# Rotary embedding: the rotated halves made by ScalarE copies instead of a TensorE product

## The chip, the cores and the metric

The kernel runs on one core of a Trainium2 chip. The metric is the time of one execution on the device, in microseconds (us). TensorE multiplies matrices, DVE (VectorE) does element-wise work and reductions, ACT (ScalarE) activations and scaled copies, POOL (GpSimd) element-wise work, and SP issues DMAs.

## What is computed

One step of an encoder layer for 512 frames of a new stream and 32 of a running one, 544 columns in all. Cut to what matters here:

```
h = rms_norm(x); z = h @ w_in          # columns: GLU a, GLU b, q, k, v, two gates
q = rope(rms_norm(q), pos); k = rope(rms_norm(k), pos)
rope: x1, x2 = halves of 64;  out = [x1*cos - x2*sin, x2*cos + x1*sin]
attention per head with two q/k pairs of width 64, block-causal mask, values of width 128
conv branch, merge with gates, w_out, residual; then a mixer with 16384 single-neuron experts
```

A head's tile holds two vectors of 64 on 128 partitions, so the half that x is paired with lies 32 partitions away: blocks 0 and 1 are exchanged, and blocks 2 and 3, and the even ones get a minus sign.

## The kernel before, in words

Everything lies transposed: channels on partitions, 544 frames along the free axis. The stage that the change touches projects h by w_in, in 72 units of 128 columns, 9 for each of 8 heads: unit 0 is q, 1 k, 2 v, 3 and 4 the GLU halves, 5 to 8 gates. A unit is 96 matmuls (16 blocks of the inner dimension, three products of high and low parts, two halves of 272 frames), written by `product` (L1616) into one of two PSUM pairs PA. Weights pass through three steps: SP loads w_raw, ACT rounds it to w_hi (L719), POOL (or DVE) subtracts to w_lo (L654, L1017). The weights of unit n + 2 are converted while unit n + 1 runs.

All small TensorE work of a head is hung into the units by hand: `head_hooks` (L1728) says behind which quarter of which unit each piece runs. The statistics of the queries run half way through unit 1 and their rotation three quarters through it; those of the keys in the same places of unit 2; the transposes of the values in unit 3; and from the first quarter of unit 3 on the attention steps: scores (L1678), weights_t (L1697), mix_values (L1714). Each waits for semaphores, and since TensorE works in order, a wait there stops the unit too.

A rotary turn, i = 0 for queries and 1 for keys, goes so. DVE evacuates the unit from PSUM to zb (L1060). ACT squares it into sq (L758), scales it by the norm's gain into xg (L759), converts the next weights (L719), and, when TensorE has summed the squares of each block of 64 (`stats`, L1651), takes the root into rstd (`std`, L739), for which the table of functions is changed in turn 0. TensorE multiplies xg by a signed permutation into the PSUM pair TO (`rot`, L1659). DVE's `rope` (L1062) takes the reciprocal of rstd (L1065), multiplies xg by the cosines (L1069), TO by the sines (L1071 to L1073), adds (L1075) and multiplies by rstd into q_t or kn_t (L1081). Between these, DVE transposes a part of the expert table (`turn`, L1020), which SP stores in DRAM (L398); each transpose waits for the store of the one two before it.

In the first three units of a head DVE has two such transposes per unit, later about one. A loop body of ACT, DVE and SP holds a pair of heads (r = 0 and 1). The last step of a head on DVE, `o_norm` (L1133), stands behind its last evacuation; in front of the second head of a pair DVE has one transpose more there than in front of the first. TO is used later in the head by the values and the attention.

Of the kernel before, what the change touches and what calls it, by code (L numbers as in the profile page):

```python
# [23 lines left out]
ACT = mybir.ActivationFunctionType  # L24
AX = mybir.AxisListType

P = 128
# [27 lines left out]
STEPS = QT + 1  # L55
# [27 lines left out]
C_COS, C_SIN, C_ID, C_BLK, C_PERM, C_ONES, C_NEG, C_END = np.cumsum([0, TP, TP, P, P, P, P, 64]).tolist()  # L83
# [29 lines left out]
def build(nc, w_all, x_t, consts, late, params, lams, keys_t, past_k, past_v, hist,  # L113
          y_t, k_t, v_n, cst_p, cst_s):
    ctx = ExitStack()
    with ctx:
# [24 lines left out]
        cst = misc.take("consts_sb", [P, C_END])  # L141
# [14 lines left out]
        xg = ay.take("xg", [P, T])  # L156
# [109 lines left out]
        S, TO = ST[:, 0:2, :], ST[:, 2:4, :]  # L266
# [8 lines left out]
        SV, TOV = S[:, :, 0:HT], TO[:, :, 0:HT]  # L275

        def two(ap):

            return ap.rearrange("p (a b) -> p a b", a=2)
# [27 lines left out]
        zb_full, z_taken = sem("zb_full"), sem("z_taken")  # L307
        sq_ready, stat_ready, std_ready = sem("sq_ready"), sem("stat_ready"), sem("std_ready")
        rot_ready, rot_taken, norm_done = sem("rot_ready"), sem("rot_taken"), sem("norm_done")
# [399 lines left out]
        def _(act):  # L709
# [31 lines left out]
            def z_slot(hp, r, i):  # L741

                h = hp * 2 + r
                n = r * ZPH + i
                j = n % 2
                un = hp * (2 * ZPH) + n

                def next_hi():
                    act.wait_ge(unit_done, un + 1)
                    hi(hp * ZPH + (n // 2 + 1), j)  # L750

                if i >= 5:
                    next_hi()
                act.wait_ge(zb_full, un + 3)
                if i in (0, 1):
                    m = h * 3 + i
                    act.wait_ge(norm_done, m + 1)
                    act.activation(sq[:, :], zb[:, j, :], ACT.Square).then_inc(sq_ready, 1)  # L758
                    act.activation(xg[:, :], zb[:, j, :], ACT.Copy, scale=par[:, P_QG + i:P_QG + i + 1]).then_inc(z_taken, 1)  # L759
                if i == ZPH - 1:  # L760
                    act.wait_ge(conv_done, h + 2)
                    act.dma_start(c_scr[bass.ds(h, 1), :, 0:TP].rearrange("a p n -> p (a n)"), c_run[:, 0:TP]).then_inc(c_stored, 16)
                    act.dma_start(c_scr[bass.ds(h, 1), :, TP:T].rearrange("a p n -> p (a n)"), c_run[:, TP + HIST:]).then_inc(c_stored, 16)
                    act.wait_ge(norm_done, h * 3 + 4)
                    act.dma_start(o_scr[bass.ds(h, 1)].rearrange("a p n -> p (a n)"), o_lo_st[:, :].bitcast(F32)).then_inc(o_stored, 16)
                if i >= 4:
                    act.activation(zb[:, j, :], zb[:, j, :], ACT.Tanh, scale=0.5).then_inc(z_taken, 1)
                if i >= 5:
                    act.wait_ge(z_taken, h * 7 + (i - 1))
                    act.dma_start(gate_scr[bass.ds(h * 2 + ((i - 5) if i < 7 else (KD + i - 7)), 1)].rearrange("a p n -> p (a n)"),  # L770
                                  zb[:, j, :]).then_inc(gate_stored[(i - 5) % 2], 16)
                if i < 5:
                    next_hi()
                if i in (0, 1):
                    act.wait_ge(stat_ready, h * 3 + (i + 2))
                    std(1.0 / DH)

# [38 lines left out]
            with act.Fori(0, NH // 2) as hp:  # L816
                own.loop(hp, per)
                for r in range(2):
                    h = hp * 2 + r
# [162 lines left out]
        def _(dve):  # L982
# [79 lines left out]
            def rope(h, i):  # L1062

                dve.wait_ge(std_ready, h * 3 + (i + 3))
                own.by(V.reciprocal(rstd[:, :], rstd[:, :]))  # L1065
                cs = ((slice(0, TP), slice(0, TP)), (slice(TP, T), slice(PAST, PAST + TS)))
                dve.wait_ge(rot_ready, h * 2 + (i + 1))
                for to, fr in cs:
                    own.by(V.tensor_tensor(xg[:, to], xg[:, to], cst[:, fr], ALU.mult))  # L1069
                s0, t0 = C_SIN, TP - HT  # L1070
                own.by(V.tensor_tensor(sq[:, 0:HT], TO[:, 0, 0:HT], cst[:, s0:s0 + HT], ALU.mult))  # L1071
                own.by(V.tensor_tensor(sq[:, HT:TP], TO[:, 1, 0:t0], cst[:, s0 + HT:s0 + TP], ALU.mult))
                V.tensor_tensor(sq[:, TP:T], TO[:, 1, t0:HT], cst[:, s0 + PAST:s0 + PAST + TS], ALU.mult).then_inc(rot_taken, 1)  # L1073
                dve.wait_ge(rot_taken, h * 2 + (i + 1))
                own.by(V.tensor_tensor(xg[:, :], xg[:, :], sq[:, :], ALU.add))  # L1075
                settle()
                if i == 0:
                    dve.wait_ge(sc_ready, h * STEPS + 1)
                else:
                    dve.wait_ge(k_stored, h * 16 + 1)  # L1080
                V.tensor_tensor((kn_t if i else q_t)[:, :], xg[:, :], rstd[:, :], ALU.mult).then_inc(norm_done, 1)  # L1081
# [397 lines left out]
            i = 0  # L1479
# [133 lines left out]
        def _(pe):  # L1613
# [16 lines left out]

            ident = cst[:, C_ID:C_ID + P]
            blk = cst[:, C_BLK:C_BLK + P]
            perm = cst[:, C_PERM:C_PERM + P]
            ones = cst[:, C_ONES:C_ONES + P]

            def spread(out, m, src, start=True, stop=True):
                for f in range(2):
                    last = mm(out[:, f, 0:HT], m, src[:, f * HT:(f + 1) * HT], start=start, stop=stop)
                return last
# [11 lines left out]
            def stats(h, i):  # L1651

                pe.wait_ge(sq_ready, h * 3 + (i + 1))
                pe.wait_ge(std_ready, h * 3 + (i + 2))
                if i == 2:
                    pe.wait_ge(exp_done, h * STEPS + STEPS + 1)
                spread(S, ones if i == 2 else blk, sq).then_inc(stat_ready, 1)

            def rot(h, i):  # L1659
                pe.wait_ge(z_taken, h * 7 + (i + 1))  # L1660
                if i == 0:
                    pe.wait_ge(o_ready, h * STEPS + 1)
                else:
                    pe.wait_ge(rot_taken, h * 2 + i)
                spread(TO, perm, xg).then_inc(rot_ready, 1)

            def values(h, j):
                pe.wait_ge(zb_full, h * ZPH + 5)
# [57 lines left out]


            def head_hooks(h, r):  # L1728
                at = {(1, 1): lambda: stats(h, 0), (1, 2): lambda: rot(h, 0),
                      (2, 1): lambda: stats(h, 1), (2, 2): lambda: rot(h, 1),  # L1730
                      (3, 1): lambda: values(h, r % 2)}
                slots = [(i, q) for i in range(3, ZPH) for q in range(4)]
                for s in range(STEPS):
                    late = 2 if s == QT - 1 else 0
                    for d, f in ((0, scores), (3 + late, weights_t), (4 + late, mix_values)):
                        key = slots[4 * s + d]
                        old = at.get(key)
                        at[key] = (lambda f=f, s=s, old=old: ((old() if old else None), f(h, s)))
                at[slots[22]] = lambda: stats(h, 2)
                return at  # L1740
# [343 lines left out]
```

## Time and profile before

| | |
|---|---|
| median of 3 runs | 3885.25 us (3883.28 to 3887.92) |
| profiled execution | 3884.83 us, span 3883.0 us |
| TensorE busy | 3784.3 us, 97% of the span, mean granted clock 0.993 |
| DVE busy | 3006.9 us, 77% |
| ACT busy | 1101.9 us, 28% |
| POOL busy | 1341.8 us, 35% |
| projection stage | from 40 to 1065 us |

The span reaches from the first instruction to the last. A matmul's end is modelled, so TensorE's busy share says little of its own; idle time before an instruction and what released it say more. In rows of the timeline the first number is the start in us, the second how long the merged instructions took, and a bracket gives the engine's idle time before them and what ended it. L1638 is the line of a helper that the statistics and the rotation share; the operand tells them apart (sq and xg).

### The profile page before, as it was taken

What the parts mean: (1) busy time and instruction counts of PE and PEld (TensorE: products, weight loads), DVE (VectorE), ACT (ScalarE), POOL (GpSimd) and SP (SyncE); (2) the same over time, 40 slices, a digit from 0 to 9 for tenths busy, and PEclk for the clock granted to TensorE, in tenths of its full rate; (3) what the DMA queues carried; (4) which work ended last, traced back from release to release, by engine and by line L of the source; (5) the groups of instructions that cost most, each with busy time, mean ns of one, the idle gap of its engine ahead of it and who ended that gap; (6) DMA issues with size and microseconds to landing.
All of it is one profiled execution on the core that took longest, in us unless ns stands there. A gap on an engine that the chain in (4) does not pass through costs nothing.

```text
span 3883.0 us, 66565 instructions
## 1 busy us (share of the span) xinstructions
PE 3784.3 (97%) x24903; PEld 3728.2 (96%) x24903; DVE 3006.9 (77%) x3608; ACT 1101.9 (28%) x1120; POOL 1341.8 (35%) x923
## 2 busy tenths in 40 slices
PE   8999999999999998999999999999999999999999
PEld 7999999999899997999999999999999999999999
DVE  6887788778755554588789999997588888887876
ACT  3333333333221112222233333332222222222222
POOL 3433334333435442455542222223033333332320
PEclk9999999999999998999999999999999999999999
DMA  7799888998889997899989999999889989898995
GB/s 275 285 322 330 308 299 297 332 332 292 299 269 300 365 402 266 294 372 357 365 328 389 389 379 388 380 386 394 289 316 346 362 316 357 316 347 317 339 351 193
DMA packets 451705, 1285.55 MB, mean 331 GB/s; under 512 B 34368, under 2 KB 258368, under 8 KB 343360
## 3 DMA queue, kind: packets, MB, share of 16 engines
q1 hardware_dynamic: 372576, 876.99, 63.1%
q0 software_dynamic: 46080, 335.56, 22.0%
q10 hardware_dynamic: 32832, 70.07, 4.7%
q8 instruction: 140, 2.29, 0.2%
q14 instruction: 77, 0.63, 0.0%
HBM read 1070.18 MB, written 345.75 MB: 365 GB/s over the span
## 4 chain that ended last, share of the span: by engine, by line
PE 42%; issue 28%; POOL 13%; DMA 10%; DVE 4%; ACT 1%; SPq 1%; POOLq 0%; DVEq 0%; ACTq 0%
PE ST L1965 18%; PE ST L1888 17%; POOL w_lo L654 13%; DMA w_raw<-w_all 4%; PE PA L1888 4%; DMA u_rows<-u_out 3%; PE ST L1941 2%; DMA rows<-v_rows,v_idx 2%; DVE w_lo L1017 2%; ACT w_hi L719 1%; SPq L492 1%; DVE PA L1525 1%; DMA rows<-u_rows,v_idx 1%; PE PA L1869 1%; DVE u_out L1032 1%
## 5 line engine op out<-in xcount | busy, mean ns | idle before, releaser
L654 POOL TENSOR_TENSOR w_lo<-w_raw,w_hi 128x512 fp32r<-128x512 f32 x588 | 811.4, 1411 | 1129.6 <-ACT w_hi L719 1085.9
L719 ACT ACTIVATE w_hi<-w_raw 128x2048 fp32r<-128x2048 f32 x368 | 703.8, 1913 | 1335.6 <-PE ST L1965 513.3
L1965 PE MATMUL ST<-wt_hi,w_hi 128*128 128x384 f32 x2048 | 687.1, 336 | 13.6 <-DVE w_lo L1017 13.6
L1965 PE MATMUL ST<-wt_lo,w_hi 128*128 128x384 f32 x2048 | 685.4, 335 | 0.0
L1965 PE MATMUL ST<-wt_hi,w_lo 128*128 128x384 f32 x2048 | 685.4, 335 | 0.0
L1017 DVE TENSOR_TENSOR w_lo<-w_raw,w_hi 128x2048 fp32r<-128x2048 f32 x219 | 501.1, 2288 | 175.3 <-ACT w_hi L719 168.0
L690 POOL DMA_INDIRECT rows<-v_rows,v_idx x160 | 322.8, 2017 | 738.5 <-DVE PA L1525 669.0
L1626 PE MATMUL PA<-h_hi,w_hi 128*128 128x272 f32 x2496 | 536.5, 296 | 4.3 <-DVE w_lo L1017 4.3
L1626 PE MATMUL PA<-h_hi,w_lo 128*128 128x272 f32 x2496 | 518.6, 289 | 0.0
L1626 PE MATMUL PA<-h_lo,w_hi 128*128 128x272 f32 x2496 | 516.8, 289 | 0.0
L1888 PE MATMUL ST<-h_hi,w_hi 128*128 128x384 f32 x1408 | 508.4, 361 | 1.2 <-DVE w_lo L1017 1.2
L1888 PE MATMUL ST<-h_hi,w_lo 128*128 128x384 f32 x1408 | 475.3, 338 | 0.0
L1888 PE MATMUL ST<-h_lo,w_hi 128*128 128x384 f32 x1408 | 473.4, 336 | 0.0
L1626 PEld LDWEIGHTS PA<-h_hi,w_hi 128*128 128x128 f32 x2496 | 395.5, 189 | 23.1 <-issue 17.6
L1965 PEld LDWEIGHTS ST<-wt_hi,w_hi 128*128 128x128 f32 x2048 | 385.4, 188 | 18.0 <-DVE w_lo L1017 17.7
L1525 DVE SCALAR_TENSOR_TENSOR PA<-rows,w_g,PA 128x2048 f32<-128x2048 f32 x158 | 371.2, 2350 | 37.2 <-DMA rows<-v_rows,v_idx 36.8
L1626 PEld LDWEIGHTS PA<-h_lo,w_hi 128*128 128x128 f32 x2496 | 394.1, 189 | 0.0
L1626 PEld LDWEIGHTS PA<-h_hi,w_lo 128*128 128x128 f32 x2496 | 391.9, 190 | 0.0
L690 POOL DMA_INDIRECT rows<-u_rows,v_idx x160 | 186.2, 1164 | 577.6 <-DVE rows L1438 570.2
L1965 PEld LDWEIGHTS ST<-wt_hi,w_lo 128*128 128x128 f32 x2048 | 385.3, 188 | 0.0
L1965 PEld LDWEIGHTS ST<-wt_lo,w_hi 128*128 128x128 f32 x2048 | 385.3, 188 | 0.0
L1024 DVE STREAM_TRANSPOSE u_out<-u_in 128x2048 f32<-128x2048 f32 x104 | 239.3, 2303 | 101.7 <-DMA u_rows<-u_out 91.0
(273 smaller groups left out, 6144.8 us busy)
## 6 DMA issues: line engine op xcount, KB each, us to landing
w_raw<-w_all SPq DMA_DIRECT2D x368, 1024.0 KB, 7.8
u_in<-w_all SPq DMA_DIRECT2D x128, 1024.0 KB, 8.7
u_rows<-u_out SPq DMA_DIRECT2D x512, 256.0 KB, 7.5
v_rows<-w_all SPq DMA_DIRECT2D x128, 1024.0 KB, 10.3
a_scr<-gb ACTq DMA_DIRECT2D x128, 192.0 KB, 6.6
g_scr<-g_st ACTq DMA_DIRECT2D x24, 1024.0 KB, 11.9
gl_st<-g_scr SPq DMA_DIRECT2D x30, 768.0 KB, 10.7
a_st<-a_scr SPq DMA_DIRECT2D x30, 768.0 KB, 12.5
```

The costliest lines, as they stand in the source:

```text
L492: sp.dma_start(u_rows[UZ * NH // 2 + j, :, :, q, :].rearrange("b i n -> i b n"), u2_out[32 * q:32 * q + 32, j % 2, :].rearrange("p (b n) - ...
L654: ins = pool.tensor_tensor(w_lo[:, slot, cols], raw[:, slot, cols], w_hi[:, slot, cols].bitcast(F32), ALU.subtract)
L690: pool.indirect_dma_start(rows[j % NG][:, :], None, table, bass.IndirectOffsetOnAxis(v_idx[:, slot(j):slot(j) + 1], 0))\
L719: act.activation(w_hi[:, slot, :], raw[:, slot, :], ACT.Copy).then_inc(hi_ready, 1)
L1017: V.tensor_tensor(w_lo[:, slot, :], raw[:, slot, :], w_hi[:, slot, :].bitcast(F32), ALU.subtract)\
L1024: V.transpose(u_out[:, i % 2, :].rearrange("p (b k j) -> p k b j", b=4, k=KD), u_in[:, i % 2, :])\
L1032: V.transpose(u2_out[:, i % 2, :].rearrange("p (b k j) -> p k b j", b=4, k=KD), u2_in[:, i % 2, :])\
L1525: V.scalar_tensor_tensor(acc_g, rows[j % NG][:, :], w_g[:, bass.ds(col, 1)], acc_g, ALU.mult, ALU.add)\
L1626: last = mm(out[:, f, :], a, rhs, start=(x == 0 and y == 0), stop=(x == n - 1 and y == 2))
L1888: last = mm(dst[n], a, b[:, k, 0:NT], start=(k == 0 and y == 0), stop=(k == KD - 1 and y == 2))
L1941: last = mm(out, oh2[:, sl, :], oh1[:, sl, :], start=True, stop=True)
L1965: last = mm(PB[n % 2][:, k, :], a, r_[b][:, c, :], start=(c == 0 and y == 0), stop=(c == GRP - 1 and y == 2))
```

## The change

ScalarE makes the rotated halves: in turn i it waits as TensorE did before, then copies four blocks of 32 partitions of xg, each from the block that it is paired with, into TO, with scale -1 or 1. The copies stand behind the conversion of weights and ahead of the root. DVE's rope waits for four counts per turn. TensorE's rot, its two hooks and the permutation operand are gone (the constant itself is still loaded).

```diff
@@ scalar: z_slot
                 if i in (0, 1):
+                    act.wait_ge(z_taken, h * 7 + (i + 1))
+                    if i == 0:
+                        act.wait_ge(o_ready, h * STEPS + 1)
+                    else:
+                        act.wait_ge(rot_taken, h * 2 + i)
+                    for b in range(P // 32):
+                        act.activation(TOV[32 * b:32 * b + 32], two(xg[32 * (b ^ 1):32 * (b ^ 1) + 32, :]), ACT.Copy,
+                                       scale=(1.0 if b % 2 else -1.0)).then_inc(rot_ready, 1)
                     act.wait_ge(stat_ready, h * 3 + (i + 2))
                     std(1.0 / DH)
@@ vector: rope
-                dve.wait_ge(rot_ready, h * 2 + (i + 1))
+                dve.wait_ge(rot_ready, h * 8 + 4 * (i + 1))
@@ tensor
-            perm = cst[:, C_PERM:C_PERM + P]
-            def rot(h, i):
-                pe.wait_ge(z_taken, h * 7 + (i + 1))
-                if i == 0:
-                    pe.wait_ge(o_ready, h * STEPS + 1)
-                else:
-                    pe.wait_ge(rot_taken, h * 2 + i)
-                spread(TO, perm, xg).then_inc(rot_ready, 1)
@@ tensor: head_hooks
-                at = {(1, 1): lambda: stats(h, 0), (1, 2): lambda: rot(h, 0),
-                      (2, 1): lambda: stats(h, 1), (2, 2): lambda: rot(h, 1),
+                at = {(1, 1): lambda: stats(h, 0), (2, 1): lambda: stats(h, 1),
                       (3, 1): lambda: values(h, r % 2)}
```

## Rows read from the trace of the kernel before

**Rows 1.** The page: busy us, share of the span and instructions of each engine.
```profile
PE 3784.3 (97%) x24903; PEld 3728.2 (96%) x24903; DVE 3006.9 (77%) x3608; ACT 1101.9 (28%) x1120; POOL 1341.8 (35%) x923
```
**Rows 2.** Waits of DVE, 45 to 1065 us: us in total, times, longest.
```profile
DVE rstd L1065 <- ACT rstd L739: 22.3, 8, 4.6
```
**Rows 3.** Timeline of TensorE, head 1: start, us, instruction, idle before.
```profile
197.25 1.19 PE L1638 MATMUL ST<-sq,consts_sb 128*128 128x272 f32 x4 [1.31 <-ACT sq L758]
...
208.29 0.49 PE L1691 MATMUL ST<-kn_t,q_t 64*128 64x128 f32 x4
...
220.86 0.33 PE L1707 MATMUL ST<-consts_sb,e 128*128 128x128 f32 x1 [2.14 <-DVE e L1107]
```
**Rows 4.** Windows, fifth unit of heads 2 and 1: us, five engines, clock, DMA.
```profile
346.72:360.03 13.31, 13.31 (x107) 12.86 (x105) 9.22 (x10) 3.38 (x7) 5.11 (x4) 1.00 1.00 385
220.96:235.77 14.81, 14.81 (x105) 14.36 (x106) 9.47 (x10) 3.27 (x7) 5.11 (x4) 0.88 0.97 360
```
**Rows 5.** Timeline of TensorE around the rotation of head 2's queries.
```profile
315.21 0.41 PE L1626 MATMUL PA<-h_lo,w_hi 128*128 128x272 f32 x2
315.46 0.42 PE L1626 MATMUL PA<-h_hi,w_lo 128*128 128x272 f32 x2
...
316.88 0.41 PE L1626 MATMUL PA<-h_lo,w_hi 128*128 128x272 f32 x2
```
**Rows 6.** Groups of ScalarE by form: count, busy us, mean ns, idle before.
```profile
L798 ACT ACTIVATE a_t<-ST 128x128 f32<-128x128 f32 x8 | 2.2, 278 | 15.5 <-PE ST L1707 15.5
L782 ACT ACTIVATE v_smp<-ST 32x128 f32<-32x128 f32 x8 | 2.0, 250 | 0.0
...
L935 ACT ACTIVATE PA<-rows 128x2048 f32<-128x2048 f32 x1 | 1.9, 1872 | 0.0
```
**Rows 7.** Timeline of ScalarE, head 2, turns 0 and 1.
```profile
308.04 0.66 ACT L758 ACTIVATE sq<-zb 128x544 f32<-128x544 f32 x1 [3.44 <-DVE zb L1060]
308.60 0.74 ACT L759 ACTIVATE xg<-zb,params_sb 128x544 f32<-128x544 f32 x1
...
311.16 1.28 ACT L739 ACT_TABLE_LOAD   x1
312.92 0.72 ACT L739 ACTIVATE rstd<-ST,small 128x544 f32<-128x544 f32 x1 [0.47 <-PE ST L1638]
323.10 0.66 ACT L758 ACTIVATE sq<-zb 128x544 f32<-128x544 f32 x1 [9.47 <-DVE zb L1060]
...
326.77 0.72 ACT L739 ACTIVATE rstd<-ST,small 128x544 f32<-128x544 f32 x1 [0.56 <-PE ST L1638]
```
**Rows 8.** Timeline of DVE, head 2: the keys' last step.
```profile
333.61 0.73 DVE L1081 TENSOR_TENSOR kn_t<-xg,rstd 128x544 f32<-128x544 f32 x1
```
**Rows 9.** Timeline of TensorE, head 2: statistics of the keys, and the first scores.
```profile
325.65 1.08 PE L1638 MATMUL ST<-sq,consts_sb 128*128 128x272 f32 x4
...
336.59 0.49 PE L1691 MATMUL ST<-kn_t,q_t 64*128 64x128 f32 x4
```
**Rows 10.** Timeline of ScalarE: the first root of heads 0, 4 and 6.
```profile
60.17 0.71 ACT L739 ACTIVATE rstd<-ST,small 128x544 f32<-128x544 f32 x1 [1.55 <-PE ST L1638]
...
566.06 0.71 ACT L739 ACTIVATE rstd<-ST,small 128x544 f32<-128x544 f32 x1 [1.08 <-PE ST L1638]
...
817.23 0.71 ACT L739 ACTIVATE rstd<-ST,small 128x544 f32<-128x544 f32 x1 [0.37 <-PE ST L1638]
```
**Rows 11.** Timeline of DVE, head 1: transpose of turn 0, reciprocal of turn 1, keys.
```profile
184.91 2.31 DVE L1024 STREAM_TRANSPOSE u_out<-u_in 128x2048 f32<-128x2048 f32 x1 [7.43 <-DMA u_rows<-u_out]
...
201.45 3.51 DVE L1065 RECIPROCAL rstd<-rstd 128x544 f32<-128x544 f32 x1
...
207.26 0.73 DVE L1081 TENSOR_TENSOR kn_t<-xg,rstd 128x544 f32<-128x544 f32 x1
```
**Rows 12.** Timeline of ScalarE, head 1: the roots of turns 0 and 1.
```profile
183.04 0.72 ACT L739 ACTIVATE rstd<-ST,small 128x544 f32<-128x544 f32 x1 [1.04 <-PE ST L1638]
...
199.55 0.69 ACT L739 ACTIVATE rstd<-ST,small 128x544 f32<-128x544 f32 x1
```

## The prediction

> **What bounds the kernel now.** I read the page first. TensorE is busy in 97% of the span [rows 1], so a change in the projection stage (40 to 1065 us) counts when it moves TensorE, directly or by making it wait. Then I asked the chain of waits for DVE in that stage: eight times, 22.3 us in all, the reciprocal that opens a rotary turn waited for ScalarE's square root [rows 2]. Those are both turns of heads 0, 2, 4 and 6, called even here. In them the path from ScalarE's root over DVE to the rotated keys has no cover of its own.
>
> The odd heads look different. There TensorE itself waits: 1.31 us for the square of the keys before the second statistics product, and 2.14 us for the first attention weights ahead of the fifth unit of columns; only the scores run without idle time before them [rows 3]. The table by stage then shows what such a wait can cost behind it: the fifth unit took 14.81 us at a mean granted clock of 0.88 after the 2.14 us of idle time, and 13.31 us at 1.00 in head 2, where no such wait stood before it [rows 4]. That is 1.5 us for a stretch at 1.2 GHz instead of 2.4.
>
> **What the change removes.** One rotation on TensorE, sixteen times (8 heads, queries and keys). Two ordinary products that follow each other start 0.25 us apart (315.21, 315.46); across the rotation the distance from the pair at 315.46 to the one after next, at 316.88, is 1.42 us, where two pairs would take 0.50 [rows 5]. So a rotation costs 0.92 us of TensorE's time, its weight loads within that, and 16 of them 14.7 us. This is the most that the change can give. The PSUM pair TO is written by ScalarE now, in the same place of the order as seen by DVE; no DMA is moved, and no queue of SP or POOL gets or loses an instruction.
>
> **What it adds.** Four ScalarE copies of 32x544 per turn. No row has that form. Fewer partitions don't help: 32x128 took 250 ns where 128x128 took 278; and PSUM as the destination doesn't hurt: 128x2048 into it took 1872 ns [rows 6], 0.9 ns a column, where the square of 544 columns took 0.66 us [rows 7], 1.2 ns a column. So a copy is priced as the square of 128x544: 0.66 us long, the next one starting 0.56 us after it (308.04, 308.60) [rows 7]. Four take 3 x 0.56 + 0.66 = 2.3 us. Bounds: from below, a quarter of the partitions at a quarter of the time, 0.7 us for the four; from above 0.74 us each (the copy with a gain per partition) [rows 7] with no overlap, 3.0 us. I take 2.3, the nearest row by size.
>
> The waits that the copies carry cost nothing. The first output of the head before is ScalarE's own earlier work, and DVE's last read of TO in turn 0 lies ahead of the evacuation that ScalarE has already waited for when it squares the keys.
>
> **Where the copies lie.** Behind the conversion w_hi and ahead of the table load and the root. In turn 0 of head 2 the conversion ended at 311.16, the table load took 1.28 us, and the root then sat idle 0.47 us for the statistics [rows 7]. That idle time is the only cover: the root comes 2.3 - 0.47 = 1.8 us later. In turn 1 there is no load, and 0.56 us of idle time [rows 7]: 1.7 us later again. Behind the root DVE does the reciprocal, the rotation, a transpose, the evacuation of the next unit, and ScalarE's next square follows that; DVE was waiting for the root [rows 2], so both delays add, 3.5 us at the finished keys.
>
> **What TensorE feels, even heads.** In head 2 the keys were done at 333.61 + 0.73 = 334.34 [rows 8] and the scores started at 336.59 [rows 9]: 2.25 us of slack. TensorE stands in order, so what counts is when the scores can start: 3.5 - 2.25 = 1.25 us later than before, and everything behind them in the head moves with it. What TensorE saved by the missing rotations (1.8 us) only makes it wait longer: it reaches the second statistics at 325.65 - 0.92 = 324.73 [rows 9], the square ends at 323.76 + 1.8 = 325.56 [rows 7], 0.8 us of waiting, and at the scores some 2.2 us more.
> The other even heads have other idle times before the first root: 1.55, 1.08 and 0.37 us in heads 0, 4 and 6 [rows 10], so the first delay is 0.75, 1.2 and 1.9 us. With 1.7 for turn 1 and 2.25 of slack, taken from head 2, heads 0, 4 and 6 lose 0.2, 0.65 and 1.35 us. Together with head 2: +3.5 us.
>
> **Odd heads.** In head 1 the DVE turn starts with a transpose that waited 7.43 us for a store of rows, and ended at 184.91 + 2.31 = 187.2 [rows 11]; the reciprocal stands behind it, while the root had been done at 183.04 + 0.72 = 183.76, with 1.04 us of idle time before it [rows 12]. It comes 2.3 - 1.04 = 1.3 us later, at 185.0: hidden. The square of the keys then stays where it is, and the 0.92 us that TensorE saves before it become waiting (1.31 to 2.2 us). In turn 1 the root follows the conversion at once (199.55) [rows 12], so it ends 2.3 us later, at 202.5, against a reciprocal that began at 201.45 [rows 11]: 1.1 us later. The scores ran 0.3 us after the keys (207.26 + 0.73 to 208.29) [rows 3, 11], so they come some 0.8 us later; that eats into the 2.14 us wait for the attention weights [rows 3], whose own chain runs through a transpose that waits for another store and isn't moved. Net 0 for the position of the fifth unit. But its wait shrinks to about 1.3 us. In heads 1 and 3 (head 3's rows repeat head 1's) I count that the slow stretch behind it goes: -1.5 us each, -3 us. Heads 5 and 7 have no such stretch to lose.
>
> **The clock in the even heads** is the term that I can't settle. A wait of 2.2 us at the scores is new there, and one of 2.14 us stood ahead of a stretch at 1.2 GHz [rows 3, 4]. If it brings the same 1.5 us each time, that is 6 us; if never, 0. I take half, +3 us.
>
> **Sum.** The profiled execution took 3884.8 us, span 3883.0. 3884.8 + 3.5 - 3 + 3 = 3888.3. The median of the runs shown is 0.4 us above that execution, so 3888 stands for both.
>
> **A rule that speaks against the change.** In the trace the load starts as the conversion ends, and it and the idle time of 0.47 us account for everything up to the root [rows 7]; nothing is seen besides 1.28 us. The Trainium skill (ScalarE: Activation LUTs, "What ACT_TABLE_LOAD costs") puts a switch of tables at 1283 ns and 1380 ns of drain. By that rule the copies would expose 1.4 us more in turn 0 of each even head, an estimate from that page of 3894 us in all.
>
> **Rivals.**
> (a) *The clock falls in every even head and heads 1 and 3 keep theirs.* Place: the wait at the scores, or the one of 2.2 us at the statistics of the odd heads. Price: 3.5 + 6 = 9.5 us, 3894. It decides the sign once the granted clock falls in three even heads. For it: the row of 2.14 us. Against: 1.31 us brought none. 0.17.
> (b) *A switch of tables costs more than its load once real work stands directly before it.* Bound from above by a second load's time, 1.28 us per even head: 5.1 us, 3893. The row of head 2, where the load does follow work directly, speaks against it. 0.06.
> (c) *Copies at their upper bound.* 0.7 us more per turn, two turns, four even heads: 5.6 us, 3894. 0.08.
> (d) *Cheap copies*, by number of partitions. The four then take 0.7 us, turn 0 and 1 delay the keys by 0.3 us together, the slack covers that, and each even head keeps its 1.84 us: -7.4 - 3, 3874. Rows 6 speak against it. 0.11.
> (e) *TensorE simply gets its 14.7 us back*, the late keys not being felt: 3870. Only if the slack I read isn't what orders things. 0.03.
> That the copies don't take the rotation's place, or that the table load moves ahead of them, would leave the sum alone.
>
> **How the numbers follow.** A measurement of this kernel tells 0.2% (7.8 us) from no change. My own case, 0.55, is within it; (d) and (e) are faster, 0.14; (a), (b) and (c) slower, 0.31. The range runs from 3878, which leaves out (d) and (e), to 3897, which takes in (a) with a little of (c).
>
> **What would show it.** Right: sixteen groups of four 32x544 copies of 0.6 to 0.7 us; the first root of head 2 about 1.8 us later against its statistics; a new TensorE wait of about 2 us at the scores in even heads; the wait for attention weights in heads 1 and 3 near 1 us; projection stage as long as before within 5 us. Wrong: copies under 0.3 us, no wait at the scores, or a projection stage shorter by 7 us or more. A weight conversion or the subtraction on POOL that comes too late for the fifth unit of an even head would be a further term that I left at nothing; it follows the same delayed evacuation.

## The result, and the profile after

| | before | after |
|---|---|---|
| median of 5 runs each | 3883.28 us (3877.66 to 3887.92) | 3897.68 us (3895.92 to 3908.58) |
| ratio, 95% interval | | 1.0047 [1.0031, 1.0063] |
| span of the profiled execution | 3883.0 us | 3895.6 us |

The kernel is slower by 0.47%, more than the 0.2% that can be told from no change, and the median lies 0.7 us beyond the upper end of the range. The forecast was "the same", at 3888. Ratios and medians here and below leave out two executions of later rounds that ran in a much slower state (5849.8 and 9967.79 us, at granted clocks of 0.59 and 0.49).

The page of the changed kernel, engines and the queue that brings instructions (queue: packets, MB, share):

```profile
PE 3775.5 (97%) x24839; PEld 3719.8 (95%) x24839; DVE 3009.0 (77%) x3608; ACT 1141.8 (29%) x1184; POOL 1359.5 (35%) x923
...
q14 instruction: 92, 0.75, 0.1%
```

ScalarE has 64 instructions and 39.9 us more, TensorE 64 instructions and 8.8 us less [rows 1]. The last row looked like nothing: before, this queue had 77 packets and 0.63 MB. It turns out to matter.

The table by stage, changed kernel: the projections, then the rest. The stage is cut here from its first product to the first one of the next stage. Columns are the window, its length, busy us of PE, PEld, DVE, ACT and POOL, granted clock, DMA share, GB/s.

```profile
39.60:1060.10 1020.50, 985.82 (x7588) 954.10 (x7587) 811.45 (x871) 356.42 (x536) 394.98 (x284) 0.99 0.88 308
1060.10:3895.60 2835.50, 2770.15 (x17191) 2751.23 (x17190) 2169.90 (x2714) 766.74 (x624) 943.08 (x624) 0.99 0.91 340
```

The same view of the kernel before:

```profile
40.60:1048.70 1008.10, 990.76 (x7652) 959.34 (x7651) 807.47 (x870) 316.45 (x472) 394.89 (x284) 1.00 0.88 312
1048.70:3883.00 2834.30, 2771.48 (x17191) 2752.59 (x17189) 2171.67 (x2714) 766.75 (x624) 925.49 (x624) 0.99 0.91 340
```

12.4 of the 12.6 us lie in the projections. By heads, from the first product of one to the first of the next:

| head | 0 | 1 | 2 | 3 | 4 | 5 | 6 | 7 |
|---|---|---|---|---|---|---|---|---|
| before | 123.3 | 129.9 | 122.9 | 130.3 | 122.9 | 128.3 | 122.9 | 127.7 |
| after | 125.2 | 128.0 | 127.4 | 127.8 | 127.2 | 128.8 | 127.1 | 129.0 |

The even heads got longer by 1.9, 4.5, 4.3 and 4.2 us, 15 in all; the odd ones got shorter by 2.6 together. Heads 2, 4 and 6 lost more than twice as much as head 0. That is the first clue: these three are the ones behind a jump back in ScalarE's loop, whose body is a pair of heads.

ScalarE in head 2 after the change, its timeline (to be held against [rows 7]):

```profile
309.51 0.66 ACT L758 ACTIVATE sq<-zb 128x544 f32<-128x544 f32 x1 [5.86 <-issue]
310.08 0.73 ACT L759 ACTIVATE xg<-zb,params_sb 128x544 f32<-128x544 f32 x1
310.72 1.90 ACT L719 ACTIVATE w_hi<-w_raw 128x2048 fp32r<-128x2048 f32 x1
312.64 2.55 ACT L781 ACTIVATE ST<-xg 32x544 f32<-32x544 f32 x4
315.21 1.28 ACT L739 ACT_TABLE_LOAD   x1
316.50 0.72 ACT L739 ACTIVATE rstd<-ST,small 128x544 f32<-128x544 f32 x1
...
326.69 0.66 ACT L758 ACTIVATE sq<-zb 128x544 f32<-128x544 f32 x1 [9.47 <-DVE zb L1068]
...
332.39 0.71 ACT L739 ACTIVATE rstd<-ST,small 128x544 f32<-128x544 f32 x1
```

And DVE in the same head:

```profile
305.51 0.69 DVE L1068 TENSOR_TENSOR zb<-PA,rs 128x544 f32<-128x544 f32 x1
...
317.25 3.55 DVE L1073 RECIPROCAL rstd<-rstd 128x544 f32<-128x544 f32 x1 [8.84 <-ACT rstd L739]
...
333.14 3.55 DVE L1073 RECIPROCAL rstd<-rstd 128x544 f32<-128x544 f32 x1 [4.26 <-ACT rstd L739]
...
338.98 0.73 DVE L1089 TENSOR_TENSOR kn_t<-xg,rstd 128x544 f32<-128x544 f32 x1
```

Four copies take 2.55 us (2.3 forecast), and the root follows the table load directly. But look at the first row of ScalarE. DVE had evacuated the unit at 305.51 + 0.69 = 306.20, and the square came at 309.51, after 5.86 us of idle time that ends in "issue": for 3.3 us the engine waited for nothing that the profile shows. Before, that square waited for the evacuation, as it should [rows 7]. DVE's wait for the first root was 3.54 us before and is 8.84 now; the 5.3 us more are 3.3 of silence and 2.0 of copies. (The evacuation came 0.8 us earlier in this head than before, so that the root itself is 4.5 us later, counted from the head's first product.) In turn 1 DVE's wait was 2.23 and is 4.26, 2.0 more, copies alone.

The waits of ScalarE for its squares in the stage (total, times, longest), changed kernel:

```profile
ACT sq L758 <- DVE zb L1068: 106.9, 13, 12.4
ACT sq L758 <- issue: 17.7, 3, 5.9
```

Before, all sixteen squares waited for DVE. Now three don't, in heads 2, 4 and 6. In ScalarE's records at the end of the loop body, the time from the branch to the next instruction was 0.27, 0.25 and 0.24 us before, and 4.76, 4.85 and 4.79 us after. These gaps are called the silence below.

TensorE's waits in the stage, changed kernel, and two pieces of its timeline in head 2:

```profile
PE ST L1645 <- ACT sq L758: 21.2, 7, 3.4
PE ST L1690 <- DVE kn_t L1089: 6.7, 6, 1.6
```

```profile
327.40 2.18 PE L1645 MATMUL ST<-sq,consts_sb 128*128 128x272 f32 x4 [3.35 <-ACT sq L758]
...
340.23 0.49 PE L1690 MATMUL ST<-kn_t,q_t 64*128 64x128 f32 x4
```

The delay comes out at the second statistics, where 0.8 us had been forecast and 3.35 are seen; the pair of products then takes 2.18 us instead of 1.08 [rows 9], at the lower of the clock's two levels, and the whole unit 19.36 us at a granted clock of 0.82:

```profile
317.78:337.14 19.36, 16.01 (x103) 15.33 (x102) 14.93 (x13) 6.29 (x8) 5.02 (x4) 0.82 0.78 275
```

The scores started at 340.23. Counted from the head's first product (292.81 us, before 293.76) that is 47.4 us instead of 42.8 [rows 9], 4.6 us later. By the trace's record of the granted clock it fell in six of the eight heads (all but 1 and 3), before in two (1 and 3).

### The profile page after: what moved, and what is told of

It is laid out like the page before. It is cut to its first block, busy times and chain, and to the rows that moved or that the text cites. A ratio compares the mean times of both kernels' runs of the same rounds, so it can differ in the third digit from the quotient of the medians.

```text
span 3895.6 us, 66525 instructions
## 1 busy us (share of the span) xinstructions
PE 3775.5 (97%) x24839; PEld 3719.8 (95%) x24839; DVE 3009.0 (77%) x3608; ACT 1141.8 (29%) x1184; POOL 1359.5 (35%) x923
## 4 chain that ended last, share of the span: by engine, by line
PE 46%; issue 28%; POOL 13%; DMA 8%; DVE 3%; SPq 1%; ACT 1%; POOLq 0%; ACTq 0%; DVEq 0%
PE ST L1963 22%; PE ST L1886 17%; POOL w_lo L654 13%; PE PA L1886 4%; DMA u_rows<-u_out 3%; DMA w_raw<-w_all 3%; PE ST L1939 2%; DVE w_lo L1025 1%; DMA rows<-v_rows,v_idx 1%; SPq L492 1%; DMA rows<-u_rows,v_idx 1%; ACT w_hi L719 1%; DVE u_out L1040 1%; PE PA L1867 1%; DVE PA L1533 1%
## 5 line engine op out<-in xcount | busy, mean ns | idle before, releaser
L690 POOL DMA_INDIRECT rows<-u_rows,v_idx x160 | 201.9, 1262 | 561.2 <-DVE rows L1446 554.1
```

Of the source, the lines that this page charges most:

```text
L690: pool.indirect_dma_start(rows[j % NG][:, :], None, table, bass.IndirectOffsetOnAxis(v_idx[:, slot(j):slot(j) + 1], 0))\
```

## The experiments

The theory after this reading: ScalarE's longer loop body makes its jump back silent for nearly 5 us (A), and the late root adds to it (B). The expectations call A theory F and B theory P. The rival is that B, with its waits and the clock, does it alone, and the silence is covered. A third view was that TensorE's saved time is worth something once nothing is late.

Four kernels went first; the kernel before had a median of 3883.35 us beside them.

**The root ahead of the copies** takes B away and leaves A.

```diff
-                    (waits and four copies)
                     act.wait_ge(stat_ready, h * 3 + (i + 2))
                     std(1.0 / DH)
+                    (waits and four copies)
```

> The changed kernel, with the root in front of the four copies instead of behind them. Theory P (the copies stand on the path from the conversion to the root): the first root of head 2 comes again at once behind its table load or its statistics, the copies run beside DVE's reciprocal of 3.5 us, and DVE's wait ahead of the cosines stays under 0.3 us; the even heads lose the waits of over 3 us at the second statistics; 3878 to 3885 us. Theory F (ScalarE's longer loop body costs a refill at the loop's back edge, nothing else matters): the order of two things in the body changes nothing, ScalarE is still silent for 4 to 5 us after the branch in front of heads 2, 4 and 6, and the time stays at 3894 to 3898 us. If both hold, the gap of 4 to 5 us is still seen and the time comes to about 3882 to 3886.

Measured: 1.0002 [0.9984, 1.0019], median 3884.12; stage 1002.0 us. ScalarE in head 2:

```profile
304.38 0.66 ACT L758 ACTIVATE sq<-zb 128x544 f32<-128x544 f32 x1 [5.93 <-issue]
...
308.79 0.72 ACT L739 ACTIVATE rstd<-ST,small 128x544 f32<-128x544 f32 x1
309.53 2.55 ACT L783 ACTIVATE ST<-xg 32x544 f32<-32x544 f32 x4
```

The copies now lie beside DVE's reciprocal of 3.55 us and nobody waits for them. No loss over the kernel before can be told any more, and the silence is still there (4.84, 4.77, 4.59 us).

**Copies of two columns** keep each copy but not its work: all but the first column of each half is left out of the rotated halves (their PSUM is zeroed once).

```diff
-    act.activation(TOV[32 * b:32 * b + 32], two(xg[...]), ...)
+    act.activation(TOV[32 * b:32 * b + 32, :, 0:1], two(xg[...])[:, :, 0:1], ...)
```

> The changed kernel, where each of the four copies moves only one column of each half (2 of 544), so the number of instructions is as in the change and their duration falls from 620 ns to about 200. It leaves out most of the rotated halves, and DVE clears the PSUM pair once at the start. Theory P: the root is late by 0.8 us per turn instead of 2.55, less the idle time that was there, so 3.5 us of delay at the keys in head 2 vanish: 3880 to 3887 us. Theory F: unchanged, 3894 to 3898 us, with the silence after ScalarE's branch still at 4 to 5 us.

Measured: 1.0012 [0.9997, 1.0028], median 3884.19; stage 1008.2 us. ScalarE's group of copies, count and mean ns, here:

```profile
L781 ACT ACTIVATE ST<-xg 32x2 f32<-32x2 f32 x64 | 10.7, 167 | 1.6
```

and in the changed kernel:

```profile
L781 ACT ACTIVATE ST<-xg 32x544 f32<-32x544 f32 x64 | 39.7, 620 | 1.6
```

Even with copies of 0.74 us for the four, the kernel isn't faster than before. The forecast's rival (d) had such copies bring 10 us. Something other than the copies' length holds it back, and the silence is in this trace too (4.95, 4.63, 4.92 us). The copies' own work does count: the median is 13 us below that of the changed kernel.

**ScalarE's loop unrolled**, everything else as changed: takes A away and leaves B.

```diff
-            with act.Fori(0, NH // 2) as hp:
-                own.loop(hp, per)
+            outer = own.value()
+            for hp in range(NH // 2):
+                own.outer, own.per, own.base, own.n = outer, per, outer + hp * per, 0
```

> The changed kernel, where only ScalarE's loop over the pairs of heads is written out four times, so it has no back edge. Theory F: the silence of 4.7 us after the branch in front of heads 2, 4 and 6 is gone, the first square of these heads follows the evacuation within 0.2 us, each of them gets 2.4 us back and with it a stretch at the lower clock: 3886 to 3890 us. Theory P: the copies stay ahead of the root, the waits at the second statistics fall only to about 1 us, and what is left over the kernel before is the 4 to 6 us of my prediction. If the silence came from something other than the jump back (a late landing, a semaphore), it stays and so does the time, 3895 to 3898.

Measured: 1.0033 [1.0016, 1.0049], median 3893.05; stage 1010.4 us. ScalarE's first square in head 2 waits for DVE again:

```profile
305.15 0.66 ACT L758 ACTIVATE sq<-zb 128x544 f32<-128x544 f32 x1 [3.69 <-DVE zb L1069]
```

DVE's two reciprocals of that head, and TensorE's scores:

```profile
312.90 3.56 DVE L1074 RECIPROCAL rstd<-rstd 128x544 f32<-128x544 f32 x1 [5.57 <-ACT rstd L739]
...
328.79 3.55 DVE L1074 RECIPROCAL rstd<-rstd 128x544 f32<-128x544 f32 x1 [4.27 <-ACT rstd L739]
```

```profile
335.42 0.49 PE L1691 MATMUL ST<-kn_t,q_t 64*128 64x128 f32 x4 [1.55 <-DVE kn_t L1090]
```

This is B by itself, as the prediction worked it: 5.57 - 3.54 = 2.03 and 4.27 - 2.23 = 2.04 us (1.8 and 1.7 forecast), and a wait at the scores. The stage is 10.1 us shorter than in the changed kernel. Part of the loss was A, part is left. The median is 3 us above the 3886 to 3890 expected; the profiled execution, 3883.13 us, was the fastest of its ten, 10 us below their median.

**The kernel before with a longer body**: 24 copies of one column in ScalarE's loop body, TensorE's rotations kept. A without B.

```diff
                     std(1.0 / DH)
+                    for b in range(6):
+                        act.activation(fill[:, n:n + 1], sm[:, S_EPS:S_EPS + 1], ACT.Copy)
```

> The kernel before, with six one-column ScalarE copies into scratch behind each root: 24 more instructions in the loop body, where the change adds 22. Theory F: a silence of 3 to 5 us appears after ScalarE's branch in front of heads 2, 4 and 6 (0.3 us in the kernel before), so the first square of these heads is about 2 us later. Since the slack at the second statistics and at the scores is 1.9 and 2.25 us, that alone should cost TensorE little: 0 to 4 us, 3883 to 3888. If body length has nothing to do with it, the next instruction follows the branch within 0.4 us as before and the time is that of the kernel before within 2 us.

Measured: 0.9993 [0.998, 1.0005], median 3882.15; stage 1005.7 us. ScalarE's first square in head 2, and TensorE's statistics of the keys and scores:

```profile
305.07 0.66 ACT L759 ACTIVATE sq<-zb 128x544 f32<-128x544 f32 x1 [5.55 <-issue]
```

```profile
320.57 1.08 PE L1641 MATMUL ST<-sq,consts_sb 128*128 128x272 f32 x4
...
331.50 0.49 PE L1694 MATMUL ST<-kn_t,q_t 64*128 64x128 f32 x4
```

The silence appears (4.47, 4.74, 4.61 us) in a kernel without one rotary copy, so it comes from the length of the body and not from what the copies do. No cost can be told in the timed runs: TensorE waits neither at the statistics nor at the scores of the even heads. The 2.25 us of slack that the prediction found, and the one at the statistics, take it up. It isn't free, though: heads 2, 4 and 6 took 371.3 us together instead of 368.6, with new waits for attention weights of 0.54 and 1.11 us in heads 2 and 4.

So by the timed runs A alone costs nothing that can be told, B alone some 0.3%, and both 0.47%. The intervals are too wide to say that this is more than their sum; the profiles say it below. The next four kernels cross the two causes; the kernel before had a median of 3880.25.

**The jump moved**: the first two slots of a pair of heads go to the end of the body, so that ScalarE jumps back between its second and third slot, where it had idle time. This changes A without lengthening any code.

```diff
+            z_slot(0, 0, 0); z_slot(0, 0, 1)
-            with act.Fori(0, NH // 2) as hp:
+            with act.Fori(0, NH // 2 - 1) as hp:
                 own.loop(hp, per)
-                (all slots of both heads)
+                slots(hp, 2)
+                z_slot(hp + 1, 0, 0); z_slot(hp + 1, 0, 1)
-            own.endloop(NH // 2)
+            own.endloop(NH // 2 - 1)
+            slots(NH // 2 - 1, 2)
```

On the changed kernel:

> The changed kernel (copies ahead of the root), with ScalarE's loop cut at another place: the first two units of a pair's first head are taken out ahead of the loop and put at its end, so the jump back stands behind the root of the keys, where ScalarE has some 9 us of idle time. Nothing else changes, and the body is as long. Theory F: the silence of 4.7 us after the branch is still there but hidden; the projection stage in the profile falls from 1020.5 us to 1008 to 1012, as it did with the loop written out (1010.4), and the time to 3884 to 3888. Theory P says the same of what is left: waits of about 1.5 us at the scores in the even heads, +2 us over the kernel before. If instead the written-out loop gained by something else than the hidden jump, this stays at 1018 to 1021 us.

Measured: 1.0027 [1.0013, 1.0042], median 3889.13, 1 us above what was expected (the profiled execution, 3884.21, was 5 us below the median); stage 1011.6 us, even heads 125.1, 125.3, 124.9 and 124.9. Head 0 is as after the change, the other three have come down to it. It agrees with the unrolled loop. ScalarE behind the keys' root of head 2:

```profile
328.36 0.72 ACT L739 ACTIVATE rstd<-ST,small 128x544 f32<-128x544 f32 x1
339.01 1.91 ACT L719 ACTIVATE w_hi<-w_raw 128x2048 fp32r<-128x2048 f32 x1 [9.93 <-DVE zb L1076]
```

The silence isn't gone. From the branch at 325.86 to the next record of the loop's own line, at 332.47, pass 6.6 us (at the second jump 4.1), while three copies and a root still run. It lies within the 9.93 us in which ScalarE waits for DVE anyway.

On the kernel before, as the control:

> The control: the kernel before with only the loop's cut moved. Its silence after the branch was 0.25 us, so there is nothing to hide: projection stage 1004 to 1009 us and the time of the kernel before within 0.1%. If it is faster by more than 0.15%, the gain of the two versions above is not theirs but the cut's.

Measured: 0.9999 [0.9986, 1.0011], median 3879.94; stage 1003.5 us. Moving the jump brings nothing of its own; with 262 records a round the jump took 0.26 and 0.24 us.

On the kernel with the root first, which takes both causes away:

> Both causes taken away: the root stands ahead of the copies, and the jump back is moved to ScalarE's idle time. Theory: no wait of TensorE in the even heads at all, which each get 2 x 0.92 us back (121.1 us per even head, as head 0 of the version with the root first, against 122.9 before), odd heads 127 to 128 us as before the change or less; projection stage 994 to 999 us against 1008.1 before and 1002.0 with the root first alone; time 3870 to 3877 us, 0.2 to 0.3% faster than the kernel before. If a rival of the kind 'TensorE's saving is taken by the next wait' holds for the even heads too, the stage stays at 1002 or more.

Measured: 0.9994 [0.9979, 1.0009], median 3874.09, against 3880.25; stage 995.1 us. The median is 0.16% lower while the ratio's interval holds 1: the timed runs don't settle a gain. The even heads took 121.7, 121.6, 121.6 and 121.1 us, 1.3 to 1.8 less than before: the rotations' price at last.

The same with the loop unrolled instead:

> Root first, ScalarE's loop written out four times instead of cut elsewhere. By the profile it should be like the version with the moved cut, 994 to 999 us in the projection stage. The written-out loop of the changed kernel measured 3893 us over its runs although its profiled execution gave 3881; if straight code costs fetches in other executions, this one comes out 5 us or more above the version with the moved cut; if not, the two agree within 3 us at 3870 to 3877.

Measured: 0.998 [0.9968, 0.9992], median 3873.46; stage 993.9 us. This one beats both kernels, the one before by a little: 0.20% faster than before, and by the two ratios 0.67% faster than the change. ScalarE in head 2, then DVE, then TensorE:

```profile
301.24 0.66 ACT L758 ACTIVATE sq<-zb 128x544 f32<-128x544 f32 x1 [3.35 <-DVE zb L1069]
...
306.22 0.71 ACT L739 ACTIVATE rstd<-ST,small 128x544 f32<-128x544 f32 x1 [0.57 <-PE ST L1646]
306.96 2.55 ACT L783 ACTIVATE ST<-xg 32x544 f32<-32x544 f32 x4
```

```profile
306.97 3.55 DVE L1074 RECIPROCAL rstd<-rstd 128x544 f32<-128x544 f32 x1 [3.54 <-ACT rstd L739]
```

```profile
318.05 1.08 PE L1646 MATMUL ST<-sq,consts_sb 128*128 128x272 f32 x4
...
328.06 0.49 PE L1691 MATMUL ST<-kn_t,q_t 64*128 64x128 f32 x4
```

The reciprocal waits 3.54 us, the same as before the change; the copies end at 309.51, a microsecond before the reciprocal at 310.52; TensorE waits neither at the statistics nor at the scores.

Last, four more profiles; the kernel before had a median of 3878.74 us beside them. Two are of **the same kernels, profiled a second time** without an edit.

> The kernel before, unchanged, for a second profiled execution. My sum took 3 us off for two stretches at the lower clock in heads 1 and 3. If these belong to the kernel, they are here again and the projection stage is 1008 us; if they belonged to that one execution, they are gone and the stage is 1003 to 1006 us, as in the two variants of it so far (1003.5, 1005.7).

> The changed kernel, unchanged, for a second profiled execution. The silence of ScalarE behind its branch is 4.7 to 4.9 us again, three times. TensorE waits 3.3 us for the second square in heads 2, 4 and 6, and the clock falls behind at least three of the seven waits of over 2.4 us; stage 1017 to 1022 us.

Measured: 3884.47 and 3895.97 us, stages 1002.9 and 1022.2 us. The table by stage of the kernel before, second execution:

```profile
39.50:1042.40 1002.90, 989.47 (x7652) 958.92 (x7651) 807.06 (x871) 316.30 (x472) 395.03 (x284) 1.00 0.89 314
```

So one execution of the kernel before differs from another by 5 us in this stage; the changed kernel's two differ by 1.7. In the second execution of the kernel before head 1 took 126.5 us (129.9 in the first), and TensorE's clock fell at 470.1 us (head 3) and 698.8 us (head 5); in the first, at 221.9 (head 1) and 474.5 (head 3). The difference lies in the odd heads: 516 us together in the first, 511 in the second. Heads 2, 4 and 6 took 368.6 in both. In the second execution of the changed kernel the silence was there again (4.86, 4.81, 4.66 us), and so were TensorE's waits of 3.3 to 3.4 us at the statistics of heads 2, 4 and 6.

**Copies beside kept rotations**: the kernel before with the jump moved, and four copies of the same size ahead of the root, into the SBUF tile rstd, which the root then overwrites. The root waits for them. B without TensorE's saving.

```diff
+                    (waits for xg and for rstd to be free)
+                    for b in range(P // 32):
+                        act.activation(two(rstd[32 * b:32 * b + 32, :]), two(xg[32 * (b ^ 1):...]), ...)
+                    act.wait_ge(scratch_done, h * 8 + 4 * (i + 1))
                     act.wait_ge(stat_ready, h * 3 + (i + 2))
                     std(1.0 / DH)
```

> The kernel before with its loop cut moved, TensorE's rotations kept, and the four copies added ahead of the root all the same, into a buffer that the root then overwrites (with a wait on them in between, some 0.1 us). It does no needed work with them: it separates the late root from the rotation that left TensorE. Theory P (the start of the scores is set by the keys): the even heads get longer by 1 to 2.3 us each though nothing left TensorE, 124.5 to 125.3 us instead of 122.9, and the stage comes to 1008 to 1012 us, the same as the changed kernel with the cut moved (1011.6); time 3886 to 3890. If TensorE's removed work did count beside the late root, this version is slower than that one by 1.8 us per even head, 1017 us or more in the stage.

Measured: 1.0026 [1.001, 1.0042], median 3889.68; stage 1012.1 us. The scores in head 2:

```profile
338.03 0.49 PE L1706 MATMUL ST<-kn_t,q_t 64*128 64x128 f32 x4 [1.49 <-DVE kn_t L1096]
```

With the jump moved, the kernel that keeps its rotations has 1.0026 and the one without them 1.0027; their stages are 1012.1 and 1011.6. While the keys are late, no gain can be told from the 64 products that TensorE saves.

**Eight extra copies** in the body instead of 24:

> The kernel before with 8 one-column copies more in ScalarE's loop body instead of 24. The profile shows 261 ScalarE records per round of the kernel before, 283 of the changed one. If the silence comes once the body no longer fits into something of fixed size, it is either there in full with 8 more (4.5 to 4.8 us) or not at all (0.3 us), not a third of it; if it grows with the length, about 1.5 us.

Measured: 3880.83 us, stage 1005.5. ScalarE's first square in head 2:

```profile
306.24 0.66 ACT L759 ACTIVATE sq<-zb 128x544 f32<-128x544 f32 x1 [3.38 <-DVE zb L1063]
```

No silence at all (0.27, 0.24, 0.23 us). With 269 records a round it is absent, with 283 it is there in full; a growth in proportion to the length is ruled out.

**Why the two delays are worth more together.** Heads 2, 4 and 6, times in us from the head's first product to the end of the rotated keys and to the start of the scores, and the length of the three heads together:

| | keys done | scores start | three heads |
|---|---|---|---|
| kernel before, and its variants without silence (4 profiles) | 40.6 | 42.8 | 368.6 in each |
| A alone (24 extra copies) | 42.2 to 42.5 | 42.8 to 43.0 | 371.3 |
| B alone (unrolled, jump moved, kept rotations) | 43.3 to 44.8 | 43.4 to 44.8 | 374.6, 375.1, 376.0 |
| both (the change, 2 profiles) | 46.8 to 47.0 | 46.9 to 47.6 | 381.7, 383.1 |

The scores start at 42.8 us or, where that is later, within 0.6 us of the finished keys. A makes the keys 1.7 to 1.9 us later, within the slack of 2.25; B makes them 2.8 to 4.2 us later, and with both they are 6.2 to 6.4 us later. The slack is there only once. So A costs these heads 2.7 us, B 6.0 to 7.4, and both 13.1 and 14.5.

The stages together. The first column has the kernels where ScalarE is silent ahead of heads 2, 4 and 6; in those of the second it isn't, since the body is short or the loop unrolled, or it is silent where it waits anyway (1011.6, 995.1 and 1012.1, jump moved):

| | silence ahead of an even head | none there |
|---|---|---|
| no copies ahead of the root, rotations kept | 1005.7 | 1008.1, 1002.9, 1003.5, 1005.5 |
| root first, rotations gone | 1002.0 | 995.1, 993.9 |
| copies ahead of the root, rotations gone (the change) | 1020.5, 1022.2 | 1011.6, 1010.4 |
| copies of two columns ahead of the root, rotations gone | 1008.2 | not run |
| copies ahead of the root, rotations kept | not run | 1012.1 |

## Why the prediction was wrong

**The step that failed** stands in "What the change removes", at the words "no queue of SP or POOL gets or loses an instruction", and in "What it adds", which prices four copies and nothing else. The words are true, but they stop at SP and POOL: that ScalarE's own stream gets longer was put at nothing, without a reason. A round of its loop is 261 records before (269 with eight extra copies), and the jump back took 0.25 us; it is 283 after (285 with 24 extra), and the jump took 4.5 to 4.9 us (up to 4.95 with copies of two columns). In heads 2, 4 and 6 that put 2.9 to 3.3 us between the evacuation and the first square. By the table above the stage is 1021.3 - 1011.0 = 10.3 us longer with the silence (means of the third row). Of these, 7.5 us lie in the three heads that it stands ahead of (382.4 against 374.9); the other 2.8 lie in heads without it and needn't be its work. Without copies it cost those heads 2.7 us, with the root first 5 to 6 (370.1 against 364.2 and 365.0).

The timed runs say less sharply the same: 1.0047 with the silence, 1.0027 and 1.0033 without, so 5 to 8 us of the 18 that the ratio gives. The intervals of these ratios overlap; the 7.5 us rest on two pairs of profiled executions, and on the first root of head 2, where the same 3.3 us (8.84 against 5.57) can be read. The forecast of 3888.3 with 10.3 us added would be 3898.6, near the 3897.68 measured, but that is partly luck: the wrong credit of the next paragraph stands in it.

**The credit for the odd heads' clock** (-3 us) was the second error. Heads 1 and 3 did get shorter, by 1.9 and 2.5 us, but heads 5 and 7 got longer by 0.5 and 1.3. The second execution of the kernel before lacked the slow stretch of head 1 with nothing changed, and had one in head 5. A stretch seen in one execution isn't the kernel's to lose. That the odd heads came out 2.6 us shorter than in the first profile, with 3 forecast, is luck: the second profile of the kernel before had them at 511 us with nothing changed, the changed kernel at 513 and 514.

**The late keys of the even heads** were forecast nearly right. With the silence out of the way the scores of the four even heads started 3.9 us later in sum, in the unrolled kernel and in the one with the jump moved (3.5 forecast). The heads got longer by 6.3 and 8.2 us (3.5 and 3 for the clock forecast). In the unrolled kernel none of the 6.3 is the clock; 2.4 us come behind the scores, with waits for attention weights of 0.4 and 0.6 us in heads 4 and 6, which the sum had at nothing. Against the mean of the two profiles of the kernel before, 1005.5, the change without the silence cost 5.5 us in the whole stage. The timed runs give more to the late root, 10 to 13 us (1.0027 and 1.0033), and both kernels' profiled executions lay under their medians. What the other 5 to 7 us are stays open.

**Point by point, what held.**
- A rotation costs TensorE 0.92 us: the second unit of head 2, which held one, went from 13.85 to 12.94 us. With both causes away the even heads are 1.3 to 1.8 us shorter (jump moved) or 0.9 to 1.7 (unrolled), where two rotations make 1.84.
- Copies of 0.6 to 0.7 us: 0.62 us each. Four take 2.55 us, not 2.3, since they don't overlap as two forms of 128x544 did [rows 7]. The root came 2.0 us later in each turn of head 2 once the silence was gone, not 1.8 and 1.7.
- Keys too late for the scores in even heads: in the unrolled kernel TensorE waited 1.54 to 1.57 us there in all four. In the changed kernel the wait of 3.35 us at the statistics of heads 2, 4 and 6 took the place of most of it.
- Turn 0 hidden in odd heads: yes. TensorE's wait at the second statistics of head 1 was 2.43 us (2.2 forecast), the scores came after a wait of 1.55 us (0.8 us of delay forecast), and the wait for attention weights, forecast at 1.3, vanished behind them.
- The table load: 1.28 us at 315.21, the root at 316.50. The Trainium skill (ScalarE: Activation LUTs, "What ACT_TABLE_LOAD costs") adds 1380 ns of drain to a switch. The trace doesn't show it, though a copy stands directly before the load; the measurement decides, and rival (b) falls.
- The subtraction on POOL, left at nothing: 1.1 us of waits in the whole stage, the longest 0.4 us; 2.8 and 2.9 without the silence, ahead of the scores' own wait.

**The rivals.** The clock did fall in every even head, as rival (a) had it, and its 3894 lay nearer than the forecast. But in heads 2, 4 and 6 it fell during the wait of 3.35 us at the statistics (at 326.4, 582.4 and 838.4 us), which has this length only where the silence and the late root come together; only in head 0 did it fall behind the wait at the scores (84.1 us). And that wait doesn't always bring it: without the silence it stands in all four even heads, and the clock fell in two of them with the jump moved (84.1 and 336.7 us) and in none with the loop unrolled, where it fell in head 3 (529.9 us). What decides it is open. (c) is refuted by 0.62 us a copy. (d) is refuted: copies aren't cheap by partitions. When made cheap by leaving columns out they brought no gain either, though with the silence still there. The path by which (e) could come true was real, only not in this order: the root first and the silence out of the way gave about 11 us of the 14.7 in the stage, and 6 to 7 between the medians of the timed runs.

## What to carry to other kernels

When a change lengthens the instruction stream of an engine inside a loop, ask what its jump back will do and what stands behind it; unrolling the loop, or putting the jump where the engine waits anyway, took some 10 us of the stage back here, and 5 to 8 by the timed runs. Added work belongs behind the result that somebody waits for, beside that waiter's own work: the same four copies cost 0.3% ahead of the root and nothing that can be told behind it. And delays on one path have to be priced together, since the slack is there only once. Last, profile the kernel before twice before crediting a change with a stretch that one profile shows.

## What was not expected of the hardware

ScalarE's jump back to the start of a loop body took 0.23 to 0.27 us with 261 and with 269 records a round, and 4.5 to 4.95 us with 283 and 285, whatever the added instructions did. With the jump moved and 285 or 290 records it took 4.1 to 6.6 us, counted to the next record of the loop's own line. The queue that brings instructions moved 0.75 MB in 92 packets in the changed kernel against 0.63 MB in 77, and in head 2 three of its fetches, of 8 KB each, started at 306.3, 306.8 and 307.1 us, inside the silence. Three such fetches lie inside the silence at each of the fifteen jumps of the five profiles that have it ahead of heads 2, 4 and 6. That the body no longer fits into what the engine keeps of its instructions is the reading that this suggests; it was not tested beyond these lengths, nor on another engine, and where the body begins in the instruction stream was not varied apart from its length.

Four copies of 32x544 by ScalarE followed each other 0.64 us apart at 0.62 us each, without overlap, while the square and the scaling of 128x544 start 0.56 us apart at 0.66 [rows 7]. The number of partitions made little difference.
